# Norms by token in a two-block latent transformer: root and reciprocal of a few columns, spread by TensorE; the context norm moved ahead

## The reference

```python
def rms_norm(x, w):                       # over the 1024 features of each token
    y = xf * lax.rsqrt(jnp.mean(xf * xf, axis=-1, keepdims=True) + EPS)
    return y * w

# first block, each layer (the branches are a gated convolution, retention and gated linear attention)
x = x + rms_norm(mixer(rms_norm(x, norm_mix_pre)), norm_mix_post)
x = x + rms_norm(swiglu(rms_norm(x, norm_ffn_pre)), norm_ffn_post)

# second block, each layer; xc is the context, 256 more tokens (in layer 1 only its norm 1 is used)
mod_x = silu(c) @ ada_w[l] + ada_b[l]     # six vectors: shift, scale and gate, twice
hx = rmsnorm(x, norm1_w[l]) * (1.0 + sc1) + sh1
hc = rmsnorm(xc, norm1_w[l]) * (1.0 + sc1c) + sh1c
x = x + g1 * mix_x                        # conformer convolution, mLSTM, attention
hx = rmsnorm(x, norm2_w[l]) * (1.0 + sc2) + sh2
x = x + g2 * conv_ffn(hx, ...)
```

## Time and profile before

| | us |
|---|---|
| median of 3 runs (lowest, highest) | 2994.91 (2989.05, 2996.57) |
| the profiled execution | 2995.09 |
| its span | 2993.3 |
| TensorE busy | 2799.6 (94%) |
| weight loads of TensorE (beside its matmuls) | 2323.2 (78%) |
| VectorE (DVE) busy | 1465.2 (49%) |
| ScalarE (ACT) busy | 1307.5 (44%) |
| GpSimd (POOL) busy | 1504.4 (50%) |
| mean granted clock of TensorE | 0.969 |

### The profile page before, as it was taken

The page is one execution under the profiler, slowest core; times in us unless marked ns, Lnnn a source line. Parts: engine busy times, 40 slices in busy tenths (PEclk is TensorE's granted clock), DMA queues, the critical chain, the costliest instruction groups (busy, mean ns, idle before and its releaser), DMA issues.

```text
span 2993.3 us, 40566 instructions
## 1 busy us (share of the span) xinstructions
PE 2799.6 (94%) x16014; PEld 2323.2 (78%) x16014; DVE 1465.2 (49%) x2351; ACT 1307.5 (44%) x2026; POOL 1504.4 (50%) x628
## 2 busy tenths in 40 slices
PE   7999999989999979989999989899998999998999
PEld 6888688788878858756777767688887868888788
DVE  5576532457663247843443341432335845445655
ACT  5464444445454443353333323342433554434554
POOL 5568678456767844311223324344444424445687
PEclk9999999999999989989999999999998999999999
DMA  5358676335867523201111212223232313223455
GB/s 193 126 176 279 215 261 201 127 110 185 275 226 265 185 93 98 71 29 41 58 64 64 71 56 86 76 98 96 95 99 93 106 49 99 86 98 115 146 185 167
DMA packets 144866, 386.37 MB, mean 129 GB/s; under 512 B 11824, under 2 KB 64304, under 8 KB 144688
## 3 DMA queue, kind: packets, MB, share of 16 engines
q1 hardware_dynamic: 144688, 383.87, 38.7%
HBM read 382.77 MB, written 1.05 MB: 128 GB/s over the span
## 4 chain that ended last, share of the span: by engine, by line
issue 37%; POOL 29%; PE 28%; DVE 4%; ACT 1%; POOLq 0%; DMA 0%; DVEq 0%; ACTq 0%
POOL w_lo L929 29%; PE bank L986 8%; PE bank L990 4%; PE bank L970 3%; PE bank L972 3%; PE bank L971 3%; PE bank L1358 1%; PE bank L1328 1%; DVE sd L1786 1%; DVE bank L2194 1%; PE bank L1035 1%; PE bank L1295 1%; PE bank L1280 1%; PE bank L1073 1%; PE bank L1024 0%
## 5 line engine op out<-in xcount | busy, mean ns | idle before, releaser
L929 POOL TENSOR_TENSOR w_lo<-raw,w_hi 128x1024 fp32r<-128x1024 f32 x624 | 1504.2, 2421 | 1478.5 <-ACT w_hi L1390 1476.1
L1390 ACT ACTIVATE w_hi<-raw 128x1024 fp32r<-128x1024 f32 x624 | 655.1, 1053 | 428.3 <-PE bank L972 184.5
L970 PE MATMUL bank<-hl,w_hi 128*128 128x256 f32 (+1 forms) x2088 | 731.7, 350 | 59.3 <-DVE hl L2113 27.5
L971 PE MATMUL bank<-hl,w_hi 128*128 128x256 f32 (+1 forms) x2088 | 709.8, 340 | 0.0
L972 PE MATMUL bank<-hl,w_lo 128*128 128x256 f32 (+1 forms) x2088 | 709.6, 340 | 0.0
L970 PEld LDWEIGHTS bank<-hl,w_hi 128*128 128x128 f32 x2088 | 406.5, 195 | 125.2 <-issue 56.7
L971 PEld LDWEIGHTS bank<-hl,w_hi 128*128 128x128 f32 x2088 | 407.9, 195 | 43.7 <-issue 5.0
L972 PEld LDWEIGHTS bank<-hl,w_lo 128*128 128x128 f32 x2088 | 407.1, 195 | 40.8
L986 PE MATMUL bank<-hl,w_hi 128*128 128x512 f32 x1368 | 364.3, 397 | 14.2 <-DVE hl L2372 5.4
L986 PEld LDWEIGHTS bank<-hl,w_hi 128*128 128x128 f32 x1368 | 247.1, 190 | 63.4 <-issue 22.3
L990 PEld LDWEIGHTS bank<-hl,w_lo 128*128 128x128 f32 x1368 | 192.6, 191 | 19.5 <-DVE hl L1799 3.4
(11 more groups left out here) (290 smaller groups left out, 4232.3 us busy)
## 6 DMA issues: line engine op xcount, KB each, us to landing
raw<-stream SPq DMA_DIRECT2D x624, 512.0 KB, 3.4
spare_lo<-stream SPq DMA_DIRECT2D x32, 512.0 KB, 5.6
mix<-stream SPq DMA_DIRECT2D x32, 512.0 KB, 5.6
spare_hi<-stream SPq DMA_DIRECT2D x32, 512.0 KB, 5.6
xs<-x_rows SPq DMA_DIRECT2D x4, 256.0 KB, 4.3
xs<-ctx_rows SPq DMA_DIRECT2D x1, 1024.0 KB, 14.6
out_rows<-xs SPq DMA_DIRECT2D x8, 128.0 KB, 2.9
cst<-consts SPq DMA_DIRECT2D x1, 896.5 KB, 10.6
```

What stands on the lines that cost most here:

```text
L929: nc.gpsimd.tensor_tensor(w_lo[:, unit % SPLIT, :], raw[:, unit % RAW, :], w_hi[:, unit % SPLIT, :], ALU.subtract).then_inc(lo_ready, 1)
L970: nc.tensor.matmul(acc, wh, x[:, 0, k, c0:c1], start=k == 0, stop=False)
L971: nc.tensor.matmul(acc, wh, x[:, 1, k, c0:c1], start=False, stop=False)
L1390: nc.scalar.activation(w_hi[:, n % SPLIT, :], raw[:, n % RAW, :], ACT.Copy).then_inc(hi_ready, 1)
```

## The change

1. `token_sums` uses each squared row as the weights and one column of ones as the moving side. Each tile of 128 tokens gives one column: the sums lie by token on the partitions. `token_roots` and `token_inverses` take root and reciprocal of two columns (four for 512 tokens), and `spread_inverse` multiplies that column, broadcast, with the identity and so writes it along the columns of a whole bank (`STAT` or `X[4]`), from where DVE's row operations now read it in place of `sd`. This holds for the norms over all features, not for the heads' norms nor the query and key norms.
2. The table of the root is loaded before the last squares (`square_rows`, `square_update`, the kernel's start). At the query sums only those for i = 0 and 3 remain.
3. DVE's partial sums of squares go into the bank `STAT`, the last ones into `work`.
4. The units at POST1 and POST2 move: MID1 and MID2 hold six, three ahead of the sums of x and three among them, PRE1 two instead of five. Layer 0 has 16 in the gates and 16 in the feed-forward (14 and 15 before), layer 1 20 and 20 (17 and 20).
5. The context's norm of the second block's layer 0 is taken during the last down projection of the first block: eight squares on ACT, seven adds on DVE, one sum on TensorE behind the first tile, root, reciprocal, and the normalised, modulated rows, two per tile. The norm at the block boundary then covers the 256 latent columns.
6. The first load of constants holds ones and identity (128 KB, was 64 KB).

The diff, cut to its core:

```diff
-    counts = spread(14 if l < DEPTH - 1 else 17, GATES[4:])
-    for place, n in ((POST1, 2), (MID1, 4), (PRE1, 5)):
+    counts = spread(16 if l < DEPTH - 1 else 20, GATES[4:])
+    for place, n in ((MID1, 6), (PRE1, 2)):
         counts[place] += n
-    for place, n in enumerate(spread(15 if l < DEPTH - 1 else 20, FFNS[3:NFF - 3])):
+    for place, n in enumerate(spread(16 if l < DEPTH - 1 else 20, FFNS[3:NFF - 3])):
         counts[place] += n
     if l < DEPTH - 1:
-        counts[POST2] += 2
-        counts[MID2] += 4
+        counts[MID2] += 6
         counts[PRE2] += 2
...
+    root_col, inv_col = sd[:, T2 - 8:T2 - 4], sd[:, T2 - 4:T2]
+    def ctx_row(k):
+        return X[k % 4][:, 0:SEQ]
...
-                    sp.dma_start(ones, consts[:, 0:P]).then_inc(ones_loaded, 16)
+                    sp.dma_start(cst[:, 0:2 * P], consts[:, 0:2 * P]).then_inc(ones_loaded, 16)
...
+            def token_sums(bank, row, c0, c1, first, last):
+                for j in range(c0 // P, c1 // P):
+                    done = nc.tensor.matmul(bank[:, j:j + 1], row[:, j * P:(j + 1) * P], ones[:, 0:1],
+                                            start=first and j == c0 // P, stop=last, skip_group_check=True)
+                return done
+            def stat_free():
+                if at["stat"]:
+                    E.need(std_ready)
+                at["stat"] += 1
+            def spread_inverse(bank, c0, c1):
+                E.need(inv_ready)
+                for j in range(c0 // P, c1 // P):
+                    last = nc.tensor.matmul(bank[:, j * P:(j + 1) * P], inv_col[:, j:j + 1].to_broadcast([P, P]), ident,
+                                            start=True, stop=True)
+                last.then_inc(inv_spread, 1)
             def last_rows_sum(c0, c1):
-                row_sum(0, 2, work[:, 0, c0:c1], c0, c1)
+                E.need(sq_ready)
+                stat_free()
+                token_sums(STAT, work[:, 0, :], c0, c1, True, False)
                 E.need(sq_tile, KD)
-                nc.tensor.matmul(STAT[:, c0:c1], ones, work[:, KD - 1, c0:c1], start=False, stop=True)\
-                    .then_inc(stat_ready, 1)
-            def norm_sum(k, c0, c1):
-                row_sum(k, KD, work[:, k, c0:c1], c0, c1)
-            def norm_sums(c0, c1):
+                token_sums(STAT, work[:, KD - 1, :], c0, c1, False, True).then_inc(stat_ready, 1)
+                spread_inverse(STAT, c0, c1)
+            def norm_sums(c0, c1, bank, units=(), spread_bank=None):
+                stat_free()
+                for unit in units[:-3]:
+                    modulation_unit(unit)
                 for k in range(KD):
-                    norm_sum(k, c0, c1)
+                    E.need(sq_ready)
+                    last = token_sums(bank, work[:, k, :], c0, c1, k == 0, k == KD - 1)
+                    if k % 2 and k // 2 < len(units[-3:]):
+                        modulation_unit(units[-3:][k // 2])
+                last.then_inc(stat_ready, 1)
+                spread_inverse(spread_bank or bank, c0, c1)
...
-                modulation_at(l, POST1)
                 last_rows_sum(c0, c1)
-                modulation_at(l, MID1)
-                norm_sums(c0, c1)
+                norm_sums(c0, c1, X[4], ADA_AT[l][MID1])
                 modulation_at(l, PRE1)
                 for t in range(NFF):
                     product_halves(hl, c0, c1, 2, fresh=None if t else h_ready)
                     modulation_at(l, FFNS[t])
-                product_halves(hid, 0, SEQ, KD - 1, fresh=ff_ready)
+                product_halves(hid, 0, SEQ, 1, fresh=ff_ready)
+                if l == DEPTH - 1:
+                    pe.wait_ge(ctx_square_sum, 1)
+                    nc.tensor.matmul(STAT[:, 0:SEQ], ones, work[:, 0, 0:SEQ], start=True, stop=True).then_inc(ctx_sum, 1)
+                product_halves(hid, 0, SEQ, KD - 2)
                 product(hid, 0, SEQ)
-                modulation_at(l, POST2)
+                if l == DEPTH - 1:
+                    pe.wait_ge(ctx_root, 1)
                 last_rows_sum(c0, c1)
-                modulation_at(l, MID2)
...
-                    norm_sums(0, T2)
+                    norm_sums(SEQ, T2, X[4], spread_bank=STAT)
+                    pe.wait_ge(ctx_ready, KD)
...
-            def root(c0, c1, n, dst=sd):
-                nc.scalar.preload_act_table(ACT.Sqrt)
+            def root(c0, c1, n, dst=sd, preload=True):
+                if preload:
+                    nc.scalar.preload_act_table(ACT.Sqrt)
                 E.need(stat_ready)
                 nc.scalar.activation(dst[:, c0:c1], STAT[:, c0:c1], ACT.Sqrt, bias=eps[:, 0:1], scale=1.0 / n)\
+                    .then_inc(std_ready, 1)
...
+            def token_roots(bank, c0, c1):
+                E.need(stat_ready)
+                cols = slice(c0 // P, c1 // P)
+                nc.scalar.activation(root_col[:, cols], bank[:, cols], ACT.Sqrt, bias=eps[:, 0:1], scale=1.0 / D)\
                     .then_inc(std_ready, 1)
...
-            def square_rows():
+            def square_rows(with_ctx=False):
                 c0, c1 = LAT
+                nc.scalar.preload_act_table(ACT.Sqrt)
+                if with_ctx:
+                    act.wait_ge(ctx_loaded, 16)
+                    act.wait_ge(ff_rows, NFF * DEPTH)
+                    for k in range(KD):
+                        square(k, xs, 0, SEQ, ctx_squares)
                 for f in range(KD - 1):
                     n = next_tile()
                     E.later(tile_done, 1)
                     act.wait_ge(tile_out, n + 1)
                     square(f, mix, c0, c1, sq_tile)
+                    if with_ctx and f == 0:
+                        act.wait_ge(ctx_sum, 1)
+                        nc.scalar.activation(sd[:, 0:SEQ], STAT[:, 0:SEQ], ACT.Sqrt, bias=eps[:, 0:1], scale=1.0 / D)\
+                            .then_inc(ctx_root, 1)
+                    if with_ctx and 1 <= f <= KD // 2:
+                        act.wait_ge(mod_ready, MODS * DEPTH)
+                        for k in (2 * f - 2, 2 * f - 1):
+                            act.wait_ge(ctx_rows, k + 1)
+                            nc.scalar.activation(h_hi[:, k, 0:SEQ], ctx_row(k), ACT.Identity,
+                                                 bias=mod[:, 0, k, 0:1]).then_inc(ctx_hi, 1)
...
+                if next_norm:
+                    nc.scalar.preload_act_table(ACT.Sqrt)
...
-                    squares_of_x(0, T2)
-                root(0, T2, D)
-                split_shifted(0, l, 0)
+                    squares_of_x(SEQ, T2)
+                token_roots(STAT if l else X[4], 0 if l else SEQ, T2)
+                split_shifted(0, l, 0 if l else SEQ)
...
-                        root(c0 if i < AG else 0, T2, AD, query_roots(i))
+                        root(c0 if i < AG else 0, T2, AD, query_roots(i), i in (0, 3))
...
+            def token_inverses(c0, c1):
+                E.need(std_ready)
+                cols = slice(c0 // P, c1 // P)
+                V.reciprocal(inv_col[:, cols], root_col[:, cols]).then_inc(inv_ready, 1)
+                E.need(inv_spread)
...
-                    last = V.tensor_tensor(work[:, 0, c0:c1], work[:, 0, c0:c1], work[:, k, c0:c1], ADD)
+                    total = work[:, 0, c0:c1] if k == 1 else STAT[:, c0:c1]
+                    dst = STAT[:, c0:c1] if k < KD - 2 else work[:, 0, c0:c1]
+                    last = V.tensor_tensor(dst, total, work[:, k, c0:c1], ADD)
...
+            def add_ctx_squares():
+                for k in range(KD):
+                    dve.wait_ge(ctx_squares, k + 1)
+                    if k:
+                        total = work[:, 0, 0:SEQ] if k == 1 else ctx_row(0)
+                        last = V.tensor_tensor(ctx_row(0) if k < KD - 1 else work[:, 0, 0:SEQ], total, work[:, k, 0:SEQ], ADD)
+                        if k < KD - 1:
+                            C.do(last)
+                            C.settle()
+                last.then_inc(ctx_square_sum, 1)
+            def ctx_norm(f):
+                if f == 1:
+                    dve.wait_ge(mod_ready, MODS * DEPTH)
+                    set_gains(0)
+                    set_halves()
+                    dve.wait_ge(ctx_root, 1)
+                    C.do(V.reciprocal(X[4][:, 0:SEQ], sd[:, 0:SEQ]))
+                    C.settle()
+                for k in (2 * f - 4, 2 * f - 3):
+                    if 0 <= k < KD:
+                        dve.wait_ge(ctx_hi, k + 1)
+                        V.scalar_tensor_tensor(h_lo[:, k, 0:SEQ], ctx_row(k), mod[:, 0, k, 0:1], h_hi[:, k, 0:SEQ],
+                                               ADD, SUB).then_inc(ctx_ready, 1)
+                for k in (2 * f - 2, 2 * f - 1):
+                    if 0 <= k < KD:
+                        if k >= 4:
+                            dve.wait_ge(ctx_ready, k - 3)
+                        V.scalar_tensor_tensor(ctx_row(k), xs[:, k, 0:SEQ], gain[:, 0, k, 0:1], X[4][:, 0:SEQ],
```

(14 more changed lines are left out.)

56 lines of the change are left out of this document (30 added, 26 removed).

## The result

| | us |
|---|---|
| after, median of 4 runs (lowest, highest) | 2962.98 (2961.72, 2967.45) |
| before in the same comparison (4 runs) | 2991.98 (2987.04, 2996.57) |
| ratio, 95% interval | 0.9906 (0.9885 to 0.9927) |
| profiled execution, span, mean granted clock | 2962.84, 2961.1, 0.971 |

The account below looks back on a forecast made before the run. TensorE bounds the long streams and stands still mostly at the norms; 2.6 + 3.2 + 1.7 + 17.4 + 6.6 + 2.0 − 0.9 − 3.0 = 29.6 us off 2995.09 gives 2965.4, eight in ten 2952 to 2978.

Parts of the forecast that it names:

- the main case: Whole kernel: gains at the norms less costs, 29.6 us, to 2965.4; own range 2956 to 2976, chance 0.56.
- The chain of 2.2 us: At the norms, last square to first multiply takes 2.2 us, between 1.6 and 3.2, for new rows and for x.
- A, B, C: First block's norms after layer 0's mixer, its feed-forward and layer 1's mixer: gains of 2.6, 1.7 and 3.2 us.
- D: Norm at the block boundary, after layer 1's feed-forward: the largest term, 17.4 us gained, between 14 and 20.
- The context norm is hidden: Last down projection of the first block covers the context norm done ahead; cost 0.9 us in the sum.
- rival 2: Last down projection: ACT's 4.3 us reaches TensorE; sign, a weight-split wait over 1 us; 2971.5 us, chance 0.13.
- E, F, G: Norms in the second block: gains of 2.2, 3.0 and 1.4 us, sum 6.6, between 4 and 10.
- Start: Norm at the kernel's start: shorter root, table and reciprocal gain 2.0 us, ends 0 and 3.4.
- Six units in the streams: Six modulation units move from first-block holes into streams bound by TensorE, 0.5 us each: cost 3.0 us.
- Rival 1: TensorE's clock stays up, since units and narrow sums count as work: 9.9 us more gain, 2955.5 us, chance 0.17.
- Rival 3: Weights arrive late after A and C; some 9 us of gain there, at B and the start lost: 2974.4, chance 0.06.
- rival 4: TensorE enters streams at 1.2 GHz and stays there: 3004 us, chance 0.04; at 0.6 strength 2989, chance 0.04.

Follow-up runs that it names:

- e1: Changed kernel with the context norm taken at the block boundary again, all 512 columns by the new chain: 2981.71 us, ratio 0.9961.
- e2: Changed kernel with the norms over all features wide again (sums, root, reciprocal), context norm still ahead: 2976.73 us, ratio 0.9948.
- e8: Changed kernel with all six units ahead of the sums of x, plus unread wide filler products at the first block's norms: 2966.72 us, ratio 0.9913.
- e9: Changed kernel with the squares of x rounded to fp32r and summed in one two-column pass instead of two one-column passes: 2963.15 us, ratio 0.9903.
- e10: Changed kernel with one-pass fp32r sums of x and all six units ahead of those sums: 2957.27 us, ratio 0.9884.
- e12: Changed kernel with units ahead of the sums and fp32r one-pass sums for x and the last rows, context's sum still wide: 2955.15 us, ratio 0.9886.
- e7: Changed kernel with unread wide filler products ahead of and among the first block's sums, units' places kept: 2963.65 us, ratio 0.9911.
- e3: Changed kernel with the root's table loaded behind the last squares again, where the root is taken: 2972.65 us, ratio 0.9928.
- e11: Changed kernel with all six units ahead of the sums and four wide filler products ahead of the block boundary's sums, none among them: 2959.11 us, ratio 0.9880.
- e6: Changed kernel with all six units ahead of the sums of x and none among them: 2959.47 us, ratio 0.9892.
- e4: Changed kernel with DVE's partial sums of squares in SBUF again instead of the bank: 2976.58 us, ratio 0.9945.

## Why the prediction was right, and where it wasn't

The time, 2965.4, is within 2.4 us of the median, and the main case held. Its steps:

- **The chain of 2.2 us** held for the new rows (1.96) and failed for x: 4.38, 3.51, 5.19 and 4.27 in A to D. The step that failed is "with about 0.25 us of latency behind each group of passes": it took the last chunk's passes to start at the last square. At half clock a chunk takes 0.86 us and DVE delivers one in 0.73, so in D the passes end 2.4 us behind the last square (1083.92 against 1081.56): 0.86 for the last chunk, the rest queue and latency. In A and C the units among them add to it. My upper end, "every pass at half clock", priced one chunk, not the queue.
- **A, B, C** came out at 2.8, 3.3, 2.1 for 2.6, 1.7, 3.2 because two errors met: the second chain was priced 1.3 to 3.0 us too short, and the deductions for a cold start (2, 1.5 and 1.4 us) were too large. In A the clock was back within 0.5 us of the first product (0.61 us for that one). In B the "longer cold start" was a shorter one: the granted clock is 0.50 until 551.5, 2.3 us behind the first product (549.23), where it had been 0.50 for all of 556 to 562, 6.2 us from the first product (555.8). The sum, 8.2 for 7.5, is closer than its parts by luck.
- **D**: 17.3 for 17.4, again from errors that cancel: 15.1 us to the first product (13 forecast), 7.0 for its tile (8.5). e1 and e2 add what I hadn't separated: nearly all of it is the context norm ahead (15.7 with it and wide norms, −0.3 without it).
- **The context norm is hidden**, nearly: −1.2 for −0.9. TensorE, DVE and POOL in the last down projection:

```profile
1018.89 1.22 PE L999 MATMUL bank<-hid,w_lo 128*128 128x256 f32 x8 [0.15 <-POOL w_lo L938]
...
1026.19 0.69 DVE L1894 TENSOR_REDUCE mix<-bank 128x256 f32<-128x512 f32 x1 [7.86 <-PE bank L995]
...
1016.44 11.83 POOL L938 TENSOR_TENSOR w_lo<-raw,w_hi 128x1024 fp32r<-128x1024 f32 x5 [4.79 <-ACT w_hi L1429]
```

POOL stands still for 4.79 us behind ACT's squares, and TensorE waits 0.15: the prepared weights outlast the pause. One tile takes 8.55 us (1017.64 to 1026.19) instead of 7.69. That this went well is in part luck: in e2, e8, e9, e10 and e12 TensorE waits over 1 us for a split, the sign that I had given for rival 2, and loses 1.5 to 3.7 us more. The way there is not ACT's pause of 4.3 us, which I had priced, but the small operations on DVE, which I had left out.
- **E, F, G**: 1.6, 3.5, 0.6, together 5.7 for 6.6. **Start**: 0.6 for 2.0. The step "root, table and reciprocal in it shrink by some 3" left out that the 32 one-column passes at half clock end at 11.98, 3.0 us behind the last square. In e12 they end 0.9 us behind it, but the start gains only 1.1, since the first product then waits 4.27 us for a load of constants.
- **Six units in the streams**, 3.0: "other" without the 2.0 us of the DVE addition is −2.8. This term is no better known than that, given what the clock does by itself.
- **Rival 1**, the clock that stays up, is refuted by the windows above (0.59, 0.50, 0.52 with TensorE busy for some 90% and more), and e7 shows that its 10 us can't be bought with filler. The rule of the Trainium skill ("TensorE: Matmul & The Clock Gate", Part 1, "What's actually happening"), read as occupied time alone, fails here as it did at L1265. Rival 3 (weights late after A and C) shows nowhere: the first products behind A and C have no wait. Of rival 4 a weak form exists: from A to D TensorE is back at full clock at most 3.1 us after the first product (1087.63 to 1090.75 in D). Behind F the window 2250 to 2260 has 0.50 throughout, but so had the same place before (2283 to 2293), and F gained 3.5.

## What to carry to other kernels

A reduction as one-column matmuls makes root and reciprocal small (0.26 and 0.17 us here), but each pass costs a weight load (5.83 us of loads in the 5.90 from 1078 to 1083.9), and in this kernel the clock was at 1.2 GHz in most of them. Compare their rate at 1.2 GHz with the rate at which rows arrive, for the queue and not only for the last one. The large gain at the block boundary came from taking away work that was ready early (the context norm, 16.4 of 29 us), not from making the boundary's own arithmetic faster. A wait ahead of such passes can cost more than its length: in e3 0.89 us more of it cost 2.1 to 4.5 us in each hole from A to D. And work moved into an engine's idle time needs its small operations checked too: what each of them reads, and what runs beside it.

## What I had not expected of the hardware

- TensorE shows 5.90 busy of 5.90 us in one-column passes at a granted 0.50. A pass takes 0.13 us mostly at full clock (4.27/32 in e11, of which the last 0.9 us are at half) and 0.21 at half (6.86/32).
- The same 3.07 us wait behind the same products lets the clock fall in the trace after and not in that of e6: 2.8 us.
- The DVE operations on SBUF that begin beside a split on POOL end only behind it: additions of 128x256 took up to 2.53 us in e4 (0.42 with a bank among the inputs), an operation of 128x8 took 2.37 in e9 (0.16 otherwise), an addition of 128x512 took 2.68 before. Begun 0.02 us ahead of the split, that addition took 0.69.
- Still open: why the same wait drops the clock in one trace only, and what the down projection would give if gains and halves were set elsewhere. No run was made for either.
